# Attention scores of two units issued as one pair, and three waits elsewhere placed anew, in a one-core transformer kernel

## The chip, the cores and the metric

The kernel runs on one core of a Trainium2 chip. Its time is the device time of one launch in microseconds (us), from inputs in HBM to the output in HBM; smaller is better. Five engines work side by side, each on its own list of instructions: PE (TensorE, matrix products; PEld is its weight load), DVE (VectorE), ACT (ScalarE), POOL (GpSimd) and SP, which only issues DMAs. They wait for one another by semaphores.

## The reference, cut to what matters

Float32 throughout, 256 tokens of width 1024. Two layers, each a SwiGLU feed-forward, an attention block and a second SwiGLU; then a second block with a token mixer (mLSTM and gated linear attention) and a product-key expert layer.

```python
def hybrid_layer(x, ...):
    x = x + 0.5 * swiglu(rmsnorm(x, ffn1_norm), ffn1_w_gate, ffn1_w_up, ffn1_w_down)
    h = rmsnorm(x, mix_norm) @ w_in
    ...
    o_a = chunk_relpos_attention(a_q, a_k, a_v, a_rel_bias)      # 6 heads of 64
    o_b = dsa_attention(rope(b_q), rope(b_k), b_v, ...)          # 5 heads of 64, 64 keys selected a row
    o_c = mla_attention(c_q, c_kv, c_kr, ...)                    # 5 heads of 96
    x = x + concatenate([o_a, o_b, o_c]) @ w_out
    return x + 0.5 * swiglu(rmsnorm(x, ffn2_norm), ffn2_w_gate, ffn2_w_up, ffn2_w_down)

# each attention: s = q @ k.T * scale (+ bias or mask);  p = softmax(s);  o = p @ v
# token mixer, at its end: concatenate([sigmoid(ml_o) * head_rms(ml_h), silu(gla_r) * head_rms(gla_h)]) @ w_out
```

## The kernel before

**Matrix products.** To keep float32 accuracy each weight tile and each activation is split in a high and a low half: ACT writes the high half (`highs`, `high_part`, L272, L999), DVE the low half as the difference (`lows`, `low_part`, `low_half`, L284, L1008, L318), and PE makes three products (high by high, high by low, low by high; L326 to L328 and L1158 to L1160). Weights stream from HBM through five slots of `RAW` and two more places in `BIG`.

**The order of the work.** There is no scheduler. Each stage has one function for each engine, and their instructions stand as the code writes them. In the attention block all engines walk one list, `ORDER`, and each takes its own part of every entry.

**Attention.** The 16 heads are 16 units: 0 to 5 of kind A, 6 to 10 of kind C (98 rows deep), 11 to 15 of kind B (masked by a selection that DVE makes in eight rounds, L1214 to L1225). For a unit i the entries are:
- `score`: PE multiplies queries by keys into bank PB5 or PB4 (L1118, two products, 128 and 256 columns wide); DVE adds the bias and takes the maximum (L1294) or only takes it (L1292); ACT takes the exponential with its row sums (L1374);
- `norm`: DVE takes the reciprocal of the sums and scales the probabilities (L1303, L1307). For units 3 and 5 ACT does the scaling (L1371);
- `probs`: PE transposes the probabilities (L1132) and ACT copies them (L1382);
- `sum`, for every two units: PE multiplies by the values (L1143), ACT copies the high half (L1388), DVE takes the low half (L1312);
- `piece`: three products with the output weights (L1158 to L1160), up to three of them between two `probs`, to fill PE. `high` and `low` are halves of the output weights' tiles;
- `heads`: transposes of queries and keys by PE (L1102), copied out by ACT (L1363), 14 groups. For kinds A and B the queries of two heads lie in 128 rows. The copy is made twice, each time scaled by a column `HEAD_SCALE` that is 0.125 on 64 rows and 0 on the other 64, so that a product over 128 rows takes one head alone.

The `score` of unit i + 1 stands ahead of `norm` and `probs` of unit i. `HEADS_FOR` tells which groups a score waits for.

**First feed-forward.** For its first piece of 128 columns DVE scales the gate (L734), waits for ACT's SiLU (L818), multiplies (L738), splits (L742, L744), and PE starts the down product (L625). Between L734 and L738 DVE makes the low half of the first down tile, 2048 columns (`lows_upto(e, 3)`, L284).

**Token mixer, end.** `gla_vector` has, in this order, `update(4)`, the scaling of `OO` (L2369), `masked(1)` (L2341, for which PE's `own(1)`, L2269, waits), `update(5)`, `update(6)`, a half of the third output tile (`low_half(e, SECOND["out"][2], 1)`, L318) and `mix_turn_vector` (L2434). PE then multiplies by the output weights (`part`), the first time only when all four turned chunks are there.

Of the kernel before, what the change touches and what calls it, by code (L numbers as in the profile page):

```python
# [81 lines left out]
def build(nc, A, out):  # L82
    ctx = ExitStack()
    with ctx:
# [35 lines left out]
        HEAD_SCALE = COLS[:, 208:210]  # L120
# [252 lines left out]
        def setup_vector(e):  # L373
            e.memset(ONES[:, :], 1.0).then_inc(*ones_done.up())
            e.memset(NROW[:, :], NEG)
            e.memset(HEAD_SCALE, 0.0).then_inc(*v_step.up())
            e.wait_ge(*v_step.last())
            for x in range(2):
                e.memset(HEAD_SCALE[64 * x:64 * x + 64, x:x + 1], 0.125)
# [221 lines left out]

        def ffn_tensor(e, i):
# [12 lines left out]
            def down(f):  # L615
                w, c = FFN[i]["down"][f // 2], f % 3
                if f % 2 == 0:
                    tile_ready(e, w)
# [73 lines left out]
        def ffn_vector(e, i):  # L692
# [35 lines left out]
            for f in range(22):  # L728
# [6 lines left out]
                if i == 0 and f == 0:  # L735
                    lows_upto(e, 3)
# [9 lines left out]
                if i == 0 and f == 0:  # L746
                    condition_vector(e)
# [126 lines left out]
        AQ = Region(BIG, HN_AT, WB_AT)(6, 256)  # L874
        AQ_HALVES = AQ[:, 0:3, :], AQ[:, 3:6, :]
        BQ_HALVES = FREED[:, 0:3, :], FREED[:, 14:16, :]
# [26 lines left out]
        for dst, base, wide in ((AQ_HALVES, 0, True), (AK, 384, True), (CQ, 0, False), (CK, 0, False),  # L903
                                (BQ_HALVES, 1152, True), (BK, 1472, True)):
            if wide:
                for k0, k1 in ((0, 2), (2, 3)):
                    srcs = [H[:, b, base + k * 128:base + (k + 1) * 128] for k in range(k0, k1) for b in range(2)]
                    if dst is AK or dst is BK:
                        to = [(dst[:, k0:k1, :], 1.0)]
                    else:  # L910
                        to = [(half[:, k0:k1, :], HEAD_SCALE[:, x:x + 1]) for x, half in enumerate(dst)
                              if half.shape[1] >= k1]
                    HEADS.append((to, srcs))
# [10 lines left out]
        for h in range(6):  # L924
            PAIRS.append((AQ_HALVES[h % 2][:, h // 2, :], AK[:, h // 2, :],
# [4 lines left out]
        for h in (4, 0, 1, 2, 3):  # L930
            PAIRS.append((BQ_HALVES[h % 2][:, h // 2, :], BK[:, h // 2, :],
# [6 lines left out]
        HEADS_FOR = {6: 8, 7: 9, 9: 10}  # L938
# [6 lines left out]
        def turned_bank(i):  # L945
# [13 lines left out]
                4: [("heads", 6, 8), ("prod", 10, 1), ("heads", 8, 10)], 7: [("heads", 12, 14)]}  # L959
        NORMED_S = (3, 5)  # L960
# [3 lines left out]
        PIECES_AT = {5: 2, 6: 1, 7: 3, 8: 2, 9: 3, 10: 2, 11: 3, 12: 2, 13: 3, 14: 2, 15: 2}  # L964
# [4 lines left out]
        HIGH_AT = {7: (2, 0), 8: (2, 1), 10: (3, 0), 11: (3, 1), 12: (4, 0), 13: (4, 1), 14: (5, 0), 15: (5, 1)}  # L969
        LOW_AT = {5: (1, 0), 6: (1, 1), 10: (2, 0), 11: (2, 1), 12: (3, 0), 13: (3, 1), 14: (4, 0), 15: (4, 1)}  # L970
        pieces_ = []
        for i in range(NP):
            if i + 1 < NP:
                ORDER.append(("score", i + 1))
# [3 lines left out]
            if i > 0 and i % 2 == 0:  # L978
# [7 lines left out]
            ORDER.append(("probs", i))  # L986
            if i in HIGH_AT:
# [25 lines left out]
        def hybrid_tensor(e, l):  # L1013
# [3 lines left out]
            for what, *a in ORDER:  # L1017
# [86 lines left out]
                elif what == "score":  # L1104
                    i = a[0]
                    q, k, _, _, late = PAIRS[i]
                    if i == 0:
                        e.wait_ge(heads_read.sem, 14 * l + 4)
                    if i == 1:
                        e.wait_ge(scored.sem, 2 * l + 2)  # L1110
                        e.wait_ge(rest_in.sem, 32)
                    if i in HEADS_FOR:
                        e.wait_ge(heads_read.sem, 14 * l + HEADS_FOR[i])
                    if late:
                        e.wait_ge(heads_read.sem, 14 * l + 14)
# [57 lines left out]
        def hybrid_vector(e, l):  # L1173
# [55 lines left out]
            for what, *a in ORDER:  # L1229
# [48 lines left out]
                elif what == "score":  # L1278
# [6 lines left out]
                    if i - 1 in NORMED_S:  # L1285
                        e.wait_ge(att_exp.sem, base + i)
                        e.reciprocal(RECIP[:, (i - 1) % 2, :], EXPSUM[:, (i - 1) % 4, :])
# [12 lines left out]
                elif what == "norm" and a[0] not in NORMED_S:  # L1300
# [22 lines left out]
        def hybrid_scalar(e, l):  # L1323
# [6 lines left out]
            for what, *a in ORDER:  # L1330
# [34 lines left out]
                elif what == "score":  # L1365
                    i = a[0]
                    e.wait_ge(*att_shift.next())
                    if i - 1 in NORMED_S:
                        for b in range(2):
                            p = P_EXP[:, (i - 1) % 2, PART[b]]  # L1370
                            x = e.activation(p, p, ACT.Copy, scale=RECIP[:, (i - 1) % 2, b:b + 1])  # L1371
                        x.then_inc(*att_normed.up())
# [956 lines left out]
        def gla_vector(e):  # L2329
# [35 lines left out]
            update(4)  # L2365
            e.wait_ge(*rs_done.next())
# [91 lines left out]
        def mix_out_vector(e):  # L2458
# [29 lines left out]
            gate(0)  # L2488
            means(0)
# [4 lines left out]
            low_half(e, SECOND["out"][3], 1)  # L2494
            lower(0)
            scale(1)
            e.wait_ge(mixer_in.sem, 192)
# [32 lines left out]
        def mix_out_tensor(e):  # L2530
# [13 lines left out]
            for j in range(4):  # L2544
                if j < 3:
                    tile_ready(e, SECOND["out"][j])
                else:
                    e.wait_ge(first_low.sem, 5)
# [900 lines left out]
```

## Time and profile before

| what | value |
|---|---|
| median of 3 runs | 1921.29 us (1921.28 to 1921.61) |
| the profiled execution | 1921.31 us, of which the span from the first to the last instruction is 1919.5 us |
| mean granted TensorE clock | 0.994 |
| PE busy | 1781.0 us (93%) |
| DVE busy | 1385.5 us (72%) |
| ACT busy | 837.2 us (44%) |
| POOL busy | 303.1 us (16%) |
| chain that ended last | PE 66%, DMA 20%, DVE 9%, ACT 3% |
| the attention stages | about 275 to 342 us and 800 to 867 us |

Busy shares are means over stages with different limits: up to about 1262 us the kernel is held mostly by PE, behind it by the gathers of the expert layer. What a change is worth is read from the stage that it touches. A row of the timeline gives the start, the duration, and in brackets how long the engine had been idle and what ended that. The next instruction of an engine starts before the end that is recorded for the one before it, so what an instruction costs its queue is the step from its start to the next start.

### The profile page before, as it was taken

The numbers are of one execution on the slowest core, as the hardware profiler recorded it, in microseconds if no ns is written. First come the engines' busy times: TensorE is split into PE (matmuls) and PEld (weight loads), VectorE is DVE, ScalarE is ACT, GpSimd is POOL, SyncE is SP. The second block draws the span as 40 slices with busy tenths as digits, with TensorE's granted clock in tenths as the row PEclk, the third lists the DMA queues.
The fourth block names the chain that finished last, engine by engine and source line by source line (L and its number), as shares of the span: only waits on it lengthen the run. The fifth ranks groups of instructions, "written<-read, shape, count | busy, mean of one in ns | idle before, by whom it ended". The sixth has DMA issues, their size and how long they took to land.

```text
span 1919.5 us, 26939 instructions
## 1 busy us (share of the span) xinstructions
PE 1781.0 (93%) x10634; PEld 1408.4 (73%) x10634; DVE 1385.5 (72%) x2793; ACT 837.2 (44%) x1606; POOL 303.1 (16%) x341
## 2 busy tenths in 40 slices
PE   9999999999999999999999999989999877777776
PEld 8999997999999999969999899865555332222222
DVE  6787677779667876777787698877776577575745
ACT  6244456633353345575333654534533333333323
POOL 0000122000000002110000000033444333333330
PEclk9999999999999999999999999999999999999999
DMA  8666552567566755426775443399999999999997
GB/s 295 202 225 214 167 183 67 197 220 242 175 220 219 230 191 189 161 87 215 237 243 170 81 132 99 145 388 421 421 420 421 421 422 421 421 422 421 421 422 295
DMA packets 217654, 506.07 MB, mean 264 GB/s; under 512 B 10339, under 2 KB 167351, under 8 KB 183864
## 3 DMA queue, kind: packets, MB, share of 16 engines
q1 hardware_dynamic: 180376, 235.90, 37.4%
q0 software_dynamic: 37152, 268.45, 33.6%
q8 instruction: 84, 1.38, 0.3%
q14 instruction: 42, 0.34, 0.0%
HBM read 503.26 MB, written 1.06 MB: 263 GB/s over the span
## 4 chain that ended last, share of the span: by engine, by line
PE 66%; DMA 20%; DVE 9%; ACT 3%; issue 1%; another core or an unknown queue 0%; SPq 0%; DVEq 0%; ACTq 0%; POOLq 0%
PE PB L326 13%; PE PB L327 12%; PE PB L328 12%; DMA RAW<-in_c_experts,BIG 10%; PE PB L2793 6%; PE PB L625 4%; PE PB L627 4%; PE PB L626 4%; DMA HTF<-in_c_experts,BIG 4%; DMA BIG<-in_c_experts,BIG 3%; DMA HIF<-in_c_experts,BIG 2%; PE PB L2715 1%; DVE LOWS L284 1%; PE PB L1118 1%; DVE RAW L3057 1%
## 5 line engine op out<-in xcount | busy, mean ns | idle before, releaser
L284 DVE TENSOR_TENSOR LOWS<-RAW,HIGH 128x2048 fp32r<-128x2048 f32 (+2 forms) x131 | 301.0, 2306 | 32.1 <-ACT HIGH L272 31.5
L326 PE MATMUL PB<-HTR,HIGH 128*128 128x256 f32 (+1 forms) x1072 | 308.0, 287 | 0.4 <-DVE LOWS L304 0.4
L327 PE MATMUL PB<-HTR,HIGH 128*128 128x256 f32 (+1 forms) x1072 | 305.4, 285 | 0.0
L328 PE MATMUL PB<-HTR,LOWS 128*128 128x256 f32 (+1 forms) x1072 | 304.9, 284 | 0.0
L272 ACT ACTIVATE HIGH<-RAW 128x2048 fp32r<-128x2048 f32 (+3 forms) x138 | 263.8, 1920 | 51.0 <-DMA RAW<-in_ffn_w_up 23.6
L326 PEld LDWEIGHTS PB<-HTR,HIGH 128*128 128x128 f32 x1072 | 202.8, 189 | 4.5 <-DVE LOWS L304 0.6
L327 PEld LDWEIGHTS PB<-HTR,HIGH 128*128 128x128 f32 x1072 | 201.0, 188 | 3.6
L818 ACT ACTIVATE BIG<-BIG 128x256 f32<-128x256 f32 x88 | 36.7, 417 | 380.7 <-DVE BIG L734 380.7
L328 PEld LDWEIGHTS PB<-HTR,LOWS 128*128 128x128 f32 x1072 | 201.1, 188 | 2.1
L2793 PE MATMUL PB<-RAW,BIG 128*128 128x512 f32 x296 | 145.2, 621 | 47.9 <-ACT BIG L3163 47.9
L3152 ACT ACTIVATE BIG<-BIG 128x2 f32<-128x2 f32 (+1 forms) x132 | 26.8, 203 | 368.4 <-DVE BIG L3057 365.6
L2793 PE MATMUL PB<-HTF,BIG 128*128 128x512 f32 x304 | 142.7, 604 | 32.2 <-ACT BIG L3163 32.2
L326 PE MATMUL PB<-HIGH,HTR 128*128 128x280 f32 (+1 forms) x568 | 167.5, 295 | 1.7 <-DVE HTR L2483 0.8
L327 PE MATMUL PB<-LOWS,HTR 128*128 128x280 f32 (+1 forms) x568 | 164.0, 289 | 0.0
L328 PE MATMUL PB<-HIGH,HTR 128*128 128x280 f32 (+1 forms) x568 | 163.6, 288 | 0.0
L2793 PEld LDWEIGHTS PB<-RAW,BIG 128*128 128x128 f32 x296 | 54.4, 193 | 128.1 <-ACT BIG L3163 71.9
L2793 PE MATMUL PB<-HIF,BIG 128*128 128x512 f32 x292 | 138.1, 595 | 1.0 <-ACT BIG L3163 0.8
L3057 DVE CUSTOM_DVE_ANT_0 HIF<-HIF,PB 128x1024 f32<-128x1024 f32 x74 | 90.2, 1219 | 64.4 <-DMA HIF<-in_c_experts,BIG 64.3
L3057 DVE CUSTOM_DVE_ANT_0 RAW<-RAW,PB 128x1024 f32<-128x1024 f32 x75 | 91.5, 1220 | 62.2 <-DMA RAW<-in_c_experts,BIG 62.2
L2793 PEld LDWEIGHTS PB<-HTF,BIG 128*128 128x128 f32 x304 | 54.1, 190 | 107.2 <-ACT BIG L3163 57.3
L3057 DVE CUSTOM_DVE_ANT_0 HTF<-HTF,PB 128x1024 f32<-128x1024 f32 x76 | 92.1, 1219 | 53.7 <-DMA HTF<-in_c_experts,BIG 53.6
L326 PE MATMUL PB<-HTR,BIGR 128*128 128x256 f32 x384 | 110.1, 287 | 0.0
(488 smaller groups left out, 4042.9 us busy)
## 6 DMA issues: line engine op xcount, KB each, us to landing
RAW<-in_ffn_w_up SPq DMA_DIRECT2D x32, 1024.0 KB, 5.5
RAW<-in_ffn_w_down SPq DMA_DIRECT2D x32, 1024.0 KB, 5.1
RAW<-in_ffn_w_gate SPq DMA_DIRECT2D x31, 1024.0 KB, 5.4
RAW<-in_w_in SPq DMA_DIRECT2D x22, 1120.0 KB, 5.7
RAW<-in_w_mod SPq DMA_DIRECT2D x20, 1024.0 KB, 5.3
BIG<-in_ffn_w_gate SPq DMA_DIRECT2D x12, 1024.0 KB, 5.5
BIG<-in_ffn_w_up SPq DMA_DIRECT2D x12, 1024.0 KB, 8.4
BIG<-in_ffn_w_down SPq DMA_DIRECT2D x12, 1024.0 KB, 5.0
```

The costliest lines, as they stand in the source:

```text
L272: e.activation(u.h, u.raw, ACT.Copy).then_inc(*high_done.up())
L284: e.tensor_tensor(u.l, u.raw, u.h.bitcast(F32), ALU.subtract).then_inc(*low_done.up())
L326: e.matmul(o, lh, rh, start=k == 0, stop=False)
L327: e.matmul(o, lh, rl, start=False, stop=False)
L328: last = e.matmul(o, ll, rh, start=False, stop=k == len(ls) - 1)
L625: e.matmul(o, F_AH[:, c, s], w.h[:, f % 2, q], start=f == 0, stop=False)
L626: e.matmul(o, F_AH[:, c, s], w.l[:, f % 2, q], start=False, stop=False)
L627: last = e.matmul(o, F_AL[:, c, s], w.h[:, f % 2, q], start=False, stop=f == 21)
L818: e.activation(F_SG[:, c, :], F_SG[:, c, :], ACT.Silu).then_inc(*silu_done.up())
L2793: x = e.matmul(PB[4 * b + h][:, :], DIAG[:, g % 4, :], PLACES[PLACE_OF[g]][:, 1024 + h * 512:1536 + h * 512], start=g % 128 == 0, stop=g = ...
L3057: e.tensor_tensor_reduce(out=u, in0=u, in1=H2[b], scale=1.0, scalar=0.0, op0=ALU.mult, op1=ALU.add, accum_out=AV[:, b, c:c + 1]).then_inc( ...
L3152: e.activation(AV[:, b, c:c + n], AV[:, b, c:c + n], ACT.Gelu).then_inc(*s_step.up())
```

## The change

In the attention blocks:
- the entry `score` of unit i + 1 no longer stands ahead of `norm` of unit i. From unit 2 on, the scores of units i + 1 and i + 2 (i odd) stand together behind `probs` of unit i: PE issues both units' 128-column products and then both units' 256-column products, and DVE and ACT take the two units one after the other;
- queries of kinds A and B are copied once, with the factor 0.125, and each unit multiplies on its own 64 rows (`PAIRS`, the slice `r`): rows 0 to 63 for the even head, 64 to 127 for the odd. `HEAD_SCALE` goes;
- DVE normalizes units 3 and 5 too (`NORMED_S` goes);
- `heads` 12 and 13 move from unit 7 to unit 6, one `sum` into the filling of unit 4, and pieces, `high` and `low` are dealt out anew.

In the first feed-forward the low half of the first down tile is made in two parts, one ahead of the wait for the factors, one behind the first split. In the mixer `masked(1)` stands ahead of the wait for `rs_done`, the half of the third output tile comes later, in `mix_out_vector`, the second half of the fourth as well, and PE's first `part` waits for one turned chunk at a time.

```diff
+        def first_down(e, x):
+            t = FFN[0]["down"][0]
+            ...
+            e.wait_ge(high_done.sem, t.splits)
+            e.tensor_tensor(t.l[:, x, :], t.raw[:, x, :], t.h[:, x, :].bitcast(F32),
+                            ALU.subtract).then_inc(*(low_done if x else first_low).up())
...
+            else:
+                first_down(e, 0)
             e.wait_ge(*rstd_full.next())
...
-                if i == 0 and f == 0:
-                    lows_upto(e, 3)
                 e.wait_ge(*silu_done.next())
...
                 if i == 0 and f == 0:
+                    first_down(e, 1)
                     condition_vector(e)
...
+            r = slice(64 * (h % 2), 64 * (h % 2) + 64)
+            PAIRS.append((AQ[r, h // 2, :], AK[r, h // 2, :],
...
-        HEADS_FOR = {6: 8, 7: 9, 9: 10}
+        HEADS_FOR = {6: 9, 8: 10, 10: 14}
...
-        NORMED_S = (3, 5)
...
-        PIECES_AT = {5: 2, 6: 1, 7: 3, 8: 2, 9: 3, 10: 2, 11: 3, 12: 2, 13: 3, 14: 2, 15: 2}
+        PIECES_AT = {5: 2, 6: 1, 7: 3, 8: 3, 9: 2, 10: 3, 11: 2, 12: 3, 13: 2, 14: 3, 15: 1}
...
-            if i + 1 < NP:
-                ORDER.append(("score", i + 1))
+            if i == 0:
+                ORDER.append(("score", 1))
...
             ORDER.append(("probs", i))
+            if i == 6:
+                ORDER.append(("heads", 12, 14))
+            if i % 2 and i + 1 < NP:
+                ORDER += [("scores", i + 1), ("score", i + 1), ("score", i + 2)]
...
                     for b in range(2):
-                        o = score_bank(i)[:, PART[b]]
-                        last = e.matmul(o, q[:, b * 128:(b + 1) * 128], k[:, 0:128 * (b + 1)], start=True, stop=True)
-                    last.then_inc(*att_scored.up())
+                        for i in units:
+                            q, k = PAIRS[i][0:2]
+                            last = e.matmul(score_bank(i)[:, PART[b]], q[:, b * 128:(b + 1) * 128], k[:, 0:128 * (b + 1)],
+                                            start=True, stop=True)
+                            if b:
+                                last.then_inc(*att_scored.up())
...
             update(4)
+            masked(1)
             e.wait_ge(*rs_done.next())
...
-            masked(1)
             update(5)
             update(6)
-            low_half(e, SECOND["out"][2], 1)
             mix_turn_vector(e)
...
             gate(0)
+            low_half(e, SECOND["out"][2], 1)
             means(0)
...
                 if j == 0:
-                    e.wait_ge(ht_low.sem, 8 * turn_count["p"] + 4)
-                part(0, j, 0, 4)
+                    for k in range(4):
+                        e.wait_ge(ht_low.sem, 8 * turn_count["p"] + k + 1)
+                        part(0, j, k, k + 1)
+                else:
+                    part(0, j, 0, 4)
```

DVE in the first feed-forward, from the copy of the factors on, before (the 2048-wide row is the low half of the first down tile):

```order
L715 COPY BIG<-PB3 128x256
L734 TENSOR_TENSOR BIG<-PB2,BIG 128x256
L284 TENSOR_TENSOR LOWS<-RAW,HIGH 128x2048
L738 TENSOR_TENSOR BIG<-PB3,BIG 128x256
L742 CAST BIGR<-BIG 128x256
L744 TENSOR_TENSOR BIGR<-BIG,BIGR 128x256
L386 COPY CT<-COLS 128x16
```

and now:

```order
L603 TENSOR_TENSOR LOWS<-RAW,HIGH 128x1024
L723 COPY BIG<-PB3 128x256
L742 TENSOR_TENSOR BIG<-PB2,BIG 128x256
L744 TENSOR_TENSOR BIG<-PB3,BIG 128x256
L748 CAST BIGR<-BIG 128x256
L750 TENSOR_TENSOR BIGR<-BIG,BIGR 128x256
L603 TENSOR_TENSOR LOWS<-RAW,HIGH 128x1024
L381 COPY CT<-COLS 128x16
```

One row of 2048 columns between the two products with PB2 and PB3 became two rows of 1024, ahead of the copy and behind the split.

ACT in the attention block, from the exponential of unit 13 (before) and of unit 12 (now) to the copy of unit 13's transposed probabilities. `BIG,SM` rows are exponentials, `HIGH` a half of an output tile, `HTR<-PB3` the high half of the sum of units 10 and 11, `BIG<-PB3` a copy of transposed probabilities. Before:

```order
L1374 ACTIVATE BIG,SM<-PB2,SM 128x128
L1374 ACTIVATE BIG,SM<-PB2,SM 128x256
L1388 ACTIVATE HTR<-PB3 128x256
L1382 ACTIVATE BIG<-PB3 128x384
L999 ACTIVATE HIGH<-RAW 128x1024
L1374 ACTIVATE BIG,SM<-PB2,SM 128x128
L1374 ACTIVATE BIG,SM<-PB2,SM 128x256
L1382 ACTIVATE BIG<-PB3 128x384
```

and now:

```order
L1371 ACTIVATE BIG,SM<-PB2,SM 128x128
L1371 ACTIVATE BIG,SM<-PB2,SM 128x256
L1371 ACTIVATE BIG,SM<-PB2,SM 128x128
L1371 ACTIVATE BIG,SM<-PB2,SM 128x256
L1004 ACTIVATE HIGH<-RAW 128x1024
L1385 ACTIVATE HTR<-PB3 128x256
L1379 ACTIVATE BIG<-PB3 128x384
L1004 ACTIVATE HIGH<-RAW 128x1024
L1379 ACTIVATE BIG<-PB3 128x384
```

Now two exponentials and a half of an output tile stand ahead of the copy of the sum, where one exponential stood.

DVE at the same place, from the normalization of unit 12 on (reciprocal and two scalings; `ISA` rows are the bias and maximum of a score, `HTR<-PB3` the low half of the sum). Before:

```order
L1303 RECIPROCAL SM<-SM 128x2
L1307 TENSOR_SCALAR BIG<-BIG,SM 128x128
L1307 TENSOR_SCALAR BIG<-BIG,SM 128x256
L1312 TENSOR_TENSOR HTR<-PB3,HTR 128x256
L1008 TENSOR_TENSOR LOWS<-RAW,HIGH 128x1024
L1294 ISA PB2,SM<-PB2,BIG 128x128
L1294 ISA SM 128x1
L1294 ISA PB2,SM<-PB2,BIG 128x256
L1294 ISA SM 128x1
L1303 RECIPROCAL SM<-SM 128x2
L1307 TENSOR_SCALAR BIG<-BIG,SM 128x128
L1307 TENSOR_SCALAR BIG<-BIG,SM 128x256
```

and now:

```order
L1305 RECIPROCAL SM<-SM 128x2
L1309 TENSOR_SCALAR BIG<-BIG,SM 128x128
L1309 TENSOR_SCALAR BIG<-BIG,SM 128x256
L1314 TENSOR_TENSOR HTR<-PB3,HTR 128x256
L1013 TENSOR_TENSOR LOWS<-RAW,HIGH 128x1024
L1305 RECIPROCAL SM<-SM 128x2
L1309 TENSOR_SCALAR BIG<-BIG,SM 128x128
L1309 TENSOR_SCALAR BIG<-BIG,SM 128x256
L1013 TENSOR_TENSOR LOWS<-RAW,HIGH 128x1024
```

The score of unit 14 no longer stands between the low half of the sum and the normalization of unit 13; the low half of an output tile still does.

## Rows read from the trace of the kernel before

**Rows 1.** Busy time by stage, the first hybrid attention (columns as the first line has them).
```profile
core 0: us, PE busy (x) PEld busy (x) DVE busy (x) ACT busy (x) POOL busy (x), PEclk, DMA share, GB/s
...
275.00:342.00 67.00, 63.09 (x398) 50.42 (x398) 51.95 (x173) 47.89 (x121) 10.49 (x8) 1.00 0.29 95
```

**Rows 2.** Chain that ended last, first feed-forward (start us, us, what).
```profile
21.15 2.20 DVE LOWS L284
...
24.62 0.47 PE PB L625
...
27.63 0.12 PE PB L326
```

**Rows 3.** Timeline, ACT then DVE, first feed-forward (start us, us, what, [idle before]).
```profile
17.54 1.90 ACT L272 ACTIVATE HIGH<-RAW 128x2048 fp32r<-128x2048 f32 x1
...
24.47 4.49 DVE L284 TENSOR_TENSOR LOWS<-RAW,HIGH 128x2048 fp32r<-128x2048 f32 x2
...
29.77 0.43 DVE L738 TENSOR_TENSOR BIG<-PB,BIG 128x256 f32<-128x256 f32 x1 [0.48 <-ACT BIG L818]
```

**Rows 4.** Timeline of PE in the first hybrid attention.
```profile
294.02 0.87 PE L1143 MATMUL PB<-BIG 128*64 128x256 f32 x8 [0.92 <-ACT BIG L1382]
...
309.03 0.47 PE L1158 MATMUL PB<-HIGH,BIGR 128*128 128x512 f32 x1 [1.74 <-ACT HTF L1363]
...
323.74 0.82 PE L1118 MATMUL PB<-HTF 128*128 128x128 f32 x4
...
324.49 0.87 PE L1143 MATMUL PB<-BIG 128*64 128x256 f32 x8
...
326.79 0.49 PE L1132 MATMUL PB<-CST,BIG 128*128 128x128 f32 x3
...
327.11 0.82 PE L1118 MATMUL PB<-HTF 128*128 128x128 f32 x4
...
330.95 0.87 PE L1143 MATMUL PB<-BIG 128*64 128x256 f32 x8
```

**Rows 5.** Timeline of DVE there, around unit 13 (325.30 and 325.50 normalize unit 12).
```profile
324.70 0.30 DVE L1294 CUSTOM_DVE_ANT_0 PB<-PB,BIG 128x128 f32<-128x128 f32 x1 [0.50 <-PE PB L1118]
...
325.30 0.16 DVE L1303 RECIPROCAL SM<-SM 128x2 f32<-128x2 f32 x1
...
325.50 0.55 DVE L1307 TENSOR_SCALAR BIG<-BIG,SM 128x128 f32<-128x128 f32 x2
...
326.70 0.42 DVE L1312 TENSOR_TENSOR HTR<-PB,HTR 128x256 fp32r<-128x256 f32 x1 [0.65 <-ACT HTR L1388]
...
327.04 1.22 DVE L1008 TENSOR_TENSOR LOWS<-RAW,HIGH 128x1024 fp32r<-128x1024 f32 x1
...
328.17 0.29 DVE L1294 CUSTOM_DVE_ANT_0 PB<-PB,BIG 128x128 f32<-128x128 f32 x1
```

**Rows 6.** Timeline of ACT there: two pieces of it.
```profile
311.41 1.05 ACT L999 ACTIVATE HIGH<-RAW 128x1024 fp32r<-128x1024 f32 x1
...
312.36 0.36 ACT L1374 ACTIVATE BIG<-PB,SM 128x128 f32<-128x128 f32 x1
...
325.48 0.37 ACT L1374 ACTIVATE BIG<-PB,SM 128x128 f32<-128x128 f32 x1
...
326.29 0.38 ACT L1388 ACTIVATE HTR<-PB 128x256 fp32r<-128x256 f32 x1
```

**Rows 7.** Timeline of PE: the index scores on 32 rows, and what follows.
```profile
261.67 1.15 PE L1084 MATMUL PB<-BIG 32*128 32x256 f32 x16
...
262.74 0.40 PE L326 MATMUL PB<-HIGH,HTR 128*128 128x280 f32 x1
```

**Rows 8.** Timeline, PE then DVE, end of the token mixer.
```profile
1227.03 2.05 PE L2269 MATMUL PB<-BIG 128*128 128x128 f32 x16 [0.79 <-DVE BIG L2341]
...
1237.66 0.60 PE L2540 MATMUL PB<-CST,BIG 128*128 128x128 f32 x4
...
1228.93 1.23 DVE L318 TENSOR_TENSOR LOWS<-RAW,HIGH 128x1024 fp32r<-128x1024 f32 x1
```

More of the change, by code:

```diff
@@ L375, in setup_vector @@
             e.memset(NROW[:, :], NEG)
[L376 to L379, printed above, removed]
             e.memset(HALF[:, :], 0.0).then_inc(*v_step.up())
@@ L600, in mods_at @@
             return MODS[i][j - 3], f % 2
+        def first_down(e, x):
+            t = FFN[0]["down"][0]
+            assert made["low"] == t.n
+            if x:
+                made["low"] += 1
+            e.wait_ge(high_done.sem, t.splits)
+            e.tensor_tensor(t.l[:, x, :], t.raw[:, x, :], t.h[:, x, :].bitcast(F32),
+                            ALU.subtract).then_inc(*(low_done if x else first_low).up())
         def ffn_tensor(e, i):
@@ L902, in build @@
         HEADS = []
-        for dst, base, wide in ((AQ_HALVES, 0, True), (AK, 384, True), (CQ, 0, False), (CK, 0, False),
-                                (BQ_HALVES, 1152, True), (BK, 1472, True)):
+        for dst, base, wide in ((AQ, 0, True), (AK, 384, True), (CQ, 0, False), (CK, 0, False),
+                                (BQ, 1152, True), (BK, 1472, True)):
             if wide:
@@ L907, in build @@
                     srcs = [H[:, b, base + k * 128:base + (k + 1) * 128] for k in range(k0, k1) for b in range(2)]
[L908 to L913, printed above, removed]
+                    HEADS.append(([(dst[:, k0:k1, :], 0.125 if dst is AQ or dst is BQ else 1.0)], srcs))
             else:
@@ L958, in build @@
         FILL = {0: [("prod", 9, 0)], 1: [("prod", 9, 1)], 2: [("prod", 10, 0)], 3: [("begin", 10, 1), ("heads", 4, 6)],
[L959 to L960 removed]
+                4: [("heads", 6, 8), ("sum", 1), ("prod", 10, 1), ("heads", 8, 10)]}
         BEGUN = [tuple(a) for f in FILL.values() for what, *a in f if what == "begin"]
         SELECT_AT = {0: (0,), 1: (1,), 2: (2,), 3: (3,), 4: (4,), 6: (5,), 7: (6,), 8: (7,)}
[L964 removed]
+        PIECES_AT = {5: 2, 6: 1, 7: 3, 8: 3, 9: 2, 10: 3, 11: 2, 12: 3, 13: 2, 14: 3, 15: 1}
         PIECE_ORDER = {0: [], 1: [("piece", m, 1, h) for m in range(2) for h in range(2)] +
@@ L977, in build @@
                 pieces_ += PIECE_ORDER[(i - 3) // 2]
-            if i > 0 and i % 2 == 0:
+            if i > 0 and i % 2 == 0 and i != 4:
                 ORDER.append(("sum", i // 2 - 1))
@@ L1103, in hybrid_tensor @@
                         last.then_inc(*heads_turned.up())
[L1104 to L1107, printed above, removed]
+                elif what == "scores" or (what == "score" and a[0] < 2):
+                    units = (a[0], a[0] + 1) if what == "scores" else (a[0],)
+                    if a[0] == 0:
                         e.wait_ge(heads_read.sem, 14 * l + 4)
-                    if i == 1:
+                    if a[0] == 1:
                         e.wait_ge(scored.sem, 2 * l + 2)
                         e.wait_ge(rest_in.sem, 32)
[L1112 to L1115, printed above, removed]
+                    if a[0] in HEADS_FOR:
+                        e.wait_ge(heads_read.sem, 14 * l + HEADS_FOR[a[0]])
                     for b in range(2):
-                        o = score_bank(i)[:, PART[b]]
-                        last = e.matmul(o, q[:, b * 128:(b + 1) * 128], k[:, 0:128 * (b + 1)], start=True, stop=True)
-                    last.then_inc(*att_scored.up())
+                        for i in units:
[4 more added lines that the diff above has]
+                                last.then_inc(*att_scored.up())
                 elif what == "probs":
@@ L1299, in hybrid_vector @@
                         selection(r_)
-                elif what == "norm" and a[0] not in NORMED_S:
+                elif what == "norm":
                     i = a[0]
@@ L1367, in hybrid_scalar @@
                     e.wait_ge(*att_shift.next())
[L1368 to L1372, printed above, removed]
                     for b in range(2):
@@ L2493, in mix_out_vector @@
             means(1)
-            low_half(e, SECOND["out"][3], 1)
             lower(0)
             scale(1)
+            low_half(e, SECOND["out"][3], 1)
             e.wait_ge(mixer_in.sem, 192)
```

22 lines of the change are left out of this document (9 added, 13 removed).

## Prediction

> **What bounds the kernel now.** I read the stage table first, since the busy shares are means. In the first attention stage PE is busy 63.09 of 67.00 us [rows 1]: it holds the stage, and all its waits together are 3.9 us. The page has PE on 66% of the chain that ended last, and it stays the bound up to the gathers behind 1262 us. So what the change brings or costs is PE's idle time, plus any change in PE's own steps. Then I read the chain and the timelines at the three places of the change. In the first feed-forward the chain leaves PE: a DVE row of 2.20 us stands in it, and PE's down product starts at 24.62 [rows 2]. In the attention PE has two large waits, 0.92 at 294.02 and 1.74 at 309.03, and from unit 8 on hardly any [rows 4]. At the end of the mixer PE waits 0.79 for a DVE mask [rows 8].
>
> The sum is made against the profiled execution, 1921.31 us, which is the median (1921.29) to 0.02. From no change a measurement of this kernel tells about 0.2%, so faster means below 1917.4 and slower above 1925.1.
>
> **First feed-forward.** The row of 2.20 goes from between DVE's two products [rows 2]. Its first half, 1.13 by the step of a row of that size (327.04 to 328.17, [rows 5]), can start when ACT's high half ends, 17.54 + 1.90 = 19.44 [rows 3], and ends at 20.6. DVE was idle there, but the copy of the factors comes some 0.4 later for it. What is late next is the SiLU, which the row of 2.20 had covered: where nothing covers it, DVE waits 0.48 for it behind a product of about 0.42, so 0.9 (the row at 29.77, [rows 3]). At L738 the sum is 23.35 (the end of 21.15 + 2.20) - 2.20 + 0.4 + 0.5, where 0.5 is the part of the 0.9 that isn't the product itself: 22.05. PE starts the down product 1.3 earlier, at 23.3. It doesn't keep all of it. The down product ends 3.0 later (27.63 - 24.62, [rows 2]), at 26.3, and the gate tile behind it needs its low half, which on DVE now stands behind the second half. Before, that low half was made from 24.47, 2.2 long (4.49 for two, [rows 3]), to 26.7, hidden. Now it starts at 24.47 - 1.3 + 1.13 = 24.3 and ends at 26.5, so PE goes on at 26.6 where it was at 27.63. Gain 1.0. The bounds are 0.3 (if all of the 1.13 is paid again) and 1.3. PE is the bound from here on, so it is carried through.
>
> **Attention, what goes.** Numbers are of the first layer; the second has the same list.
> - The wait of 1.74 [rows 4] is a piece of unit 7 that came right behind heads 12 and 13, whose copies ACT had to finish. They move one unit ahead. -1.7.
> - The wait of 0.92 at the first sum [rows 4], with ACT's copy at its end. The sum moves into the filling of a later unit, behind pieces. -1.1 with the smaller wait behind it (from both sides: 0.5 and 1.3).
> - Scores on 64 rows. A score now is four products, 128 and 256 columns twice, on 128 rows, and costs 0.75 (323.74 to 324.49, [rows 4]). A pair of them costs 1.5. No row shows 64 rows. The nearest are the index scores on 32: 16 products of 256 columns in 1.07 (261.67 to 262.74, [rows 7]), where 0.75 for 768 columns makes 4.0 for those 4096. That is 3.7 times as fast with four row groups, so they run side by side. For two groups I take that a pair costs 0.9 and saves 0.6; the bounds are 0 (nothing side by side) and 0.75 (a full half). Only pairs of kinds A and B have both groups, 2/3, 4/5, 12/13 and 14/15: the pairs with unit 6 to 10 save nothing, 10/11 with them. -1.2 ahead of unit 8, -1.2 behind.
> - One copy for a group of queries instead of two, and no memsets for `HEAD_SCALE`: nothing, ACT is busy 47.89 of 67.00 [rows 1] and PE doesn't wait there, once the 1.74 is gone. If that cover is gone too, it is a gain.
>
> What comes new ahead of unit 8: unit 3 is normalized on DVE behind a selection round and not on ACT, and the first piece waits for heads 9. I estimate 0.8 for each, about the size of the wait of 0.92 that an ACT copy left, between 0 and 1.6. With -0.3 for the smaller waits around unit 5 the part up to unit 7 makes -1.7 - 1.1 - 1.2 - 0.3 + 1.6 = -2.7. The score of unit 8 stands no longer in this part but in the next (-0.7 here): -3.4.
>
> **Attention, what comes: a loop through three engines.** Before, the score of unit i + 1 stood a whole unit ahead of the transposes that need it. Now both scores of a pair are issued behind unit i's transposes, and those of unit i + 2 must be through DVE and ACT one unit of PE's later. The order shows what stands between: on ACT two exponentials and a half tile ahead of the copy of the sum, and on DVE the low half of the sum and a half tile ahead of the second normalization. One turn, from the start of a pair's scores to the start of the next pair's:
> - score start to DVE's end, 323.74 to the next row on DVE at 324.70, 0.96 (up to the start of the maximum), and from there to the exponential 0.78 (to 325.48) [rows 4 to 6];
> - the exponentials, a step of 0.81 each (325.48 to 326.29, [rows 6]), 1.62; the half tile, 0.95 (311.41 to 312.36, [rows 6]);
> - the copy of the sum until DVE takes it, 0.41 (326.29 to 326.70), the low half 0.34 (to 327.04), the half tile 1.13 (to 328.17) [rows 5, 6];
> - the normalization 0.75 (325.30 to 325.50, and 0.55, [rows 5]), about 0.1 for PE to take it up, the transposes 0.32 (326.79 to 327.11, [rows 4]).
>
> Together 7.4. Before, two units took 6.46 from score to score (324.49 to 330.95 by the sums behind them, [rows 4]), held by PE; with side-by-side scores PE's own work would be 5.9. So the loop is longer than the work and PE waits 1.5 a turn, mostly at the transposes of units 9, 11 and 13. Pair 8/9 has no overlap and a selection round on DVE in place of the half tile; I take 8.2. Loss: 8.2 + 7.4 + 7.4 - 3 x 6.46 = 3.6 to the scores of 14/15, and 0.3 behind them, 3.9.
>
> Net for a layer: -3.4 + 3.9 = +0.5, for both +1.0. From both sides: if half of the new waits don't come, -2.9 a layer; if the row groups don't overlap, +2.4 a layer more (four pairs, 0.6 each), less where the loop hides it.
>
> A rule of the Trainium skill speaks against the scores on 64 rows. TensorEngine Tiling (Array Packing), section Key Properties, says that a change of the tiling mode, not of the tile alone, drains TensorE. The trace shows a switch out of 32 rows at 262.74, where the product behind took 0.40 as recorded, and the 16 products took 1.07 with the switch in them [rows 7]; that leaves no room for a drain of more than some 0.1. By the rule each of the seven pairs and the first scores would pay at entry and exit, 16 a layer and 3.2 us in all at 0.1; the forecast would be 1923.4, still within 0.2%.
>
> **Mixer, end.** With `masked(1)` ahead of the scaling, PE's `own(1)` doesn't wait 0.79 [rows 8]. DVE's half tile at 1228.93, 1.23 long [rows 8], goes from ahead of the turned chunks' input; PE's transposes at 1237.66 [rows 8] come up to 1.3 earlier. Then the half tiles stand ahead of the output's updates and I give back 0.2. Gain 1.1, bounds 0.3 (only part of it reaches the chain) and 1.4 (nothing given back); the gathers behind start earlier by as much.
>
> **Sum.** 1921.31 - 1.0 + 1.0 - 1.1 = 1920.2.
>
> **Rivals.**
> - A, the forecast: large waits in front go, a loop behind takes their place, 1920.2. Chance 0.6. For it: the lengths of the loop are all rows. Against: it is a chain of means, and a step of 0.3 in it counts six times.
> - B, the loop doesn't hold PE: PE's pieces between two `probs` cover it, and the new waits of 3.9 are half or less, -2.9 a layer on top. 1921.31 - 1.0 - 1.1 + 2 x (-2.9 + 0.5) = 1914.4; with no new waits at all, 2 x -3.4 in place of +1.0, 1912.4. Chance 0.25. For it: ACT and DVE have 19 and 15 us without work in the stage [rows 1]. Against: work is missing there, order isn't.
> - C, slower: the two groups of 64 rows don't run side by side. Then PE's own work stays 6.46 a turn, less of it waits, and four pairs a layer give back 0.6: 1920.2 + 4.8 = 1925.0, and above 1925.1 where a drain or one more late copy of 0.1 comes to it; it decides from a pair's cost of 1.5 on. Chance 0.12. Against: 32 rows overlap [rows 7].
> - D, the edits elsewhere bring nothing, since later waits take them up: 1921.31 + 1.0 = 1922.3. Chance 0.03.
>
> **Numbers.** A lies within 0.2% but for a tenth. B is faster nearly always. C is half slower. Faster 0.28, the same 0.63, slower 0.09. The range reaches to B with halved waits and to C: 1914.4 to 1925.0; A's own is 1917.0 to 1923.5.
>
> **What would show it.** In the trace of the changed kernel: the down product of the first feed-forward at 23.3, and the gate tile behind it at 26.6 after a short wait for DVE. No wait over 0.5 at the first sum and behind heads 12 and 13. A pair of scores of kind A or B in 0.9 from start to next start; 1.5 makes it C. Waits of 1 to 2 us for DVE's normalization at the transposes of units 9, 11 and 13, idle time of the stage about 8 us instead of 3.9; 5 or less makes it B. `own(1)` without a wait, and the mixer's transposes some 1.2 nearer to it. The prediction is wrong if the stage's length changes by more than 2.5 us, or if the two stages differ by more than 1.

## The result, and the profile after

The changed kernel took 1926.79 us (median of 7 runs, 1925.29 to 1929.25), before 1921.31 in the same session; ratio 1.0028, 95% interval 1.0018 to 1.0037. It is slower by 5.5 us, against a forecast of 1920.2, 1.1 faster. The profiled execution (1926.79 us, span 1925.0) is the median. Beside the loss the spread is wide: 4.0 from lowest to highest, where the 7 executions of before have 0.6 (18 to 27 of them in later sessions 1.4 to 2.9, without one execution of 4529 us, which no ratio counts).

The two small edits did what was forecast. PE in the first feed-forward (start us, us, engine, line, what, [idle before <- what ended it]):

```profile
23.11 0.47 PE L631 MATMUL PB<-HIGH,BIGR 128*128 128x512 f32 x1 [0.25 <-DVE BIGR L750]
26.43 0.39 PE L325 MATMUL PB<-HTR,HIGH 128*128 128x256 f32 x1 [0.30 <-DVE LOWS L283]
```

The down product starts at 23.11 where it started at 24.62 [rows 2], and the gate tile behind it waits 0.30 for DVE's low half: on the timeline of before that tile started at 27.47, so the gain is 1.04. Some of it is lost again further on: the last index scores of the first layer start 0.95 earlier than before. At the mixer's end:

```profile
1232.65 2.05 PE L2266 MATMUL PB<-BIG 128*128 128x128 f32 x16
```

`own(1)` has no wait (0.79 in [rows 8]). PE's last transposes of the mixer's output stand 5.08 later than in [rows 8] (1242.74 against 1237.66), while PE had come into the mixer 6.48 later (1214.92 to 1221.40, both on PE's timelines). The gain there is about 1.1 by the landmark behind it (1254.23 to 1259.63, 5.40 later).

So all the loss is in the two attention stages. From the last index scores of a layer to the first transposes behind its pieces, before took 80.3 in both. The change took 82.8 in the first and 85.1 in the second. The first stage, PE, by its waits and the scores:

```profile
291.19 0.55 PE L1137 MATMUL PB<-CST,BIG 128*128 128x128 f32 x3 [1.11 <-DVE BIG L1309]
...
297.41 0.47 PE L1163 MATMUL PB<-HIGH,BIGR 128*128 128x512 f32 x1 [0.51 <-ACT HTF L1365]
...
307.35 1.48 PE L1121 MATMUL PB<-HTF 98*128 98x128 f32 x8
308.75 0.87 PE L1148 MATMUL PB<-BIG 128*64 128x256 f32 x8
...
315.33 0.55 PE L1137 MATMUL PB<-CST,BIG 128*128 128x128 f32 x3 [1.70 <-DVE BIG L1309]
315.72 2.06 PE L1121 MATMUL PB<-HTF 98*128 98x128 f32 x8
317.70 0.87 PE L1148 MATMUL PB<-BIG 128*64 128x256 f32 x8
...
323.13 0.55 PE L1137 MATMUL PB<-CST,BIG 128*128 128x128 f32 x3 [0.55 <-DVE BIG L1309]
323.61 0.93 PE L1121 MATMUL PB<-HTF 64*128 64x128 f32 x8
324.46 0.87 PE L1148 MATMUL PB<-BIG 128*64 128x256 f32 x8
...
330.70 0.55 PE L1137 MATMUL PB<-CST,BIG 128*128 128x128 f32 x3 [0.84 <-DVE BIG L1309]
331.18 0.93 PE L1121 MATMUL PB<-HTF 64*128 64x128 f32 x8
...
336.47 0.50 PE L1163 MATMUL PB<-HIGH,BIGR 128*128 128x512 f32 x1 [0.94 <-DVE BIGR L1314]
```

The whole first layer, before and then with the change (columns: stretch and length, busy time of PE, PEld, DVE, ACT and POOL, granted clock, DMA share, GB/s):

```profile
261.67:341.99 80.32, 76.41 (x518) 62.79 (x517) 64.33 (x206) 54.55 (x132) 10.49 (x8) 1.00 0.34 115
260.72:343.50 82.78, 76.40 (x518) 60.59 (x517) 66.21 (x210) 50.34 (x125) 9.90 (x8) 1.00 0.32 111
```

PE's busy time is the same, 76.41 and 76.40. The scores on 64 rows made PE's work no shorter, and the whole 2.46 is more idle time, 6.38 where it was 3.91. (The ends of PE's rows are modelled, and the first two scores, from 273.41 on, are one row of 1.91, so a short gap can be hidden in it.)

The large waits of [rows 4] are gone. In their place PE waits for DVE at the transposes of units 3, 9, 11 and 13, and at a piece behind unit 14. A pair of scores on 64 rows takes 0.85 (323.61 to 324.46), the pair 8/9 on 98 rows 1.40, and the mixed pair 10/11 takes 1.98 (315.72 to 317.70).

The second stage has the same waits, but for the one at unit 11, and something more. Stretches of 4 us (columns as above), and PE's timeline there:

```profile
840.00:844.00 4.00, 2.30 (x13) 1.54 (x12) 3.78 (x13) 1.78 (x3) 0.00 (x0) 1.00 0.81 259
844.00:848.00 4.00, 4.00 (x13) 1.99 (x14) 1.93 (x9) 1.89 (x9) 0.00 (x0) 0.51 0.00 2
848.00:852.00 4.00, 4.00 (x14) 3.15 (x14) 2.18 (x5) 1.39 (x3) 0.00 (x0) 0.64 0.00 0
```

```profile
842.77 0.55 PE L1137 MATMUL PB<-CST,BIG 128*128 128x128 f32 x3 [1.70 <-DVE BIG L1309]
843.15 2.95 PE L1121 MATMUL PB<-HTF 98*128 98x128 f32 x8
846.04 1.55 PE L1148 MATMUL PB<-BIG 128*64 128x256 f32 x8
```

Behind the wait of 1.70 the granted clock goes to 0.51, which is the lower of TensorE's two levels (1.2 GHz): the same pair takes 2.89 and not 1.98, the sum behind it 1.47 and not 0.80. The layer is 2.33 longer for it, net of the wait at unit 11 that it hides. Before has a wait of 1.74 in the first stage [rows 4] and of 1.73 in the second, and no such stretch in either. Behind about 1280 us, where the kernel is held by the gathers, every profiled execution has such stretches, before's too (a granted clock of 0.50 from 1612 to 1616, for instance); the counts below are for the attention stages only.

### The profile page after: what moved, and what is told of

Same layout as the page of the kernel before. It is cut to its first block, busy times and chain, and to the rows that moved or that the text cites. A ratio compares the mean times of both kernels' runs of the same rounds, so it can differ in the third digit from the quotient of the medians.

```text
span 1925.0 us, 26932 instructions
## 1 busy us (share of the span) xinstructions
PE 1789.2 (93%) x10634; PEld 1409.0 (73%) x10634; DVE 1388.9 (72%) x2799; ACT 829.5 (43%) x1592; POOL 303.3 (16%) x341
## 4 chain that ended last, share of the span: by engine, by line
PE 64%; DMA 20%; DVE 10%; ACT 5%; issue 1%; another core or an unknown queue 0%; SPq 0%; DVEq 0%; ACTq 0%
PE PB L325 12%; PE PB L326 12%; PE PB L327 12%; DMA RAW<-in_c_experts,BIG 10%; PE PB L2793 6%; PE PB L631 4%; PE PB L633 4%; PE PB L632 4%; DMA HTF<-in_c_experts,BIG 4%; DMA BIG<-in_c_experts,BIG 3%; DMA HIF<-in_c_experts,BIG 2%; PE PB L2715 1%; ACT BIG L1371 1%; DVE LOWS L283 1%; DVE RAW L3057 1%
```

## Experiments

Times are medians, with the ratio to the kernel before and its interval. "Layer" is the length measured as above, first and second, in the profiled execution. Which side of the change costs was asked first: each part alone.

**The two small edits alone.** The attention hunks of the diff are taken back.

> The kernel before with only the two small edits of the change: the first feed-forward and the end of the mixer. The attention stays as it was. The trace of the change shows PE 1.04 ahead behind the first feed-forward (27.47 to 26.43) and 1.08 gained in the mixer. If these two are worth what they show and the attention is all that was lost: 1921.3 - 2.1 = 1919.2, with a spread as small as that of before (0.6 from lowest to highest). Rival: the gains in front are taken up by later waits or the clock falls for another reason than the attention: 1921 or more.

1919.56 (1919.2 to 1920.05), ratio 0.9992 (0.9983 to 1.0001), layers 80.3 and 80.3. At the landmark behind the mixer PE is 1.90 earlier than before (1252.33 for 1254.23), and 1.6 arrives at the end, against 2.1 forecast. The gain is not clear of noise by itself, but the spread is small and the loss is not here.

**The attention part alone.** The hunks of the feed-forward and of the mixer are taken back.

> The kernel before with the attention part of the change alone. The two other edits alone gained 1.6. If the parts add up: 1926.8 + 1.6 = 1928.4, with the spread of 3 to 4 of the changed kernel, each attention stage 2.4 longer than before and one or both longer still by a slow stretch of TensorE's clock. If the slow clock came from where the edits moved the stages in time: a small spread and 1926.1 (1921.3 + 2 x 2.4).

1929.03 (1927.80 to 1931.01), ratio 1.0041 (1.0027 to 1.0055). The parts add up to about 0.4: 7.4 for this part and -1.6 for the other make 5.8, and the change measured 5.5. Here the slow stretch stood in the first stage (layer 83.6, granted clock 0.87 and 0.70 at 316 to 324) and none in the second (82.8): it belongs to neither layer. It cost only 0.76, where the one in the change's second stage cost 2.33.

**The change once more**, unedited.

> The changed kernel once more, unedited, for the spread of its times beside the run with two filler products (1924.2 to 1926.3 in 11 runs). If idle time in the loop lets the clock fall in most executions, but not in all: a median of 1926.8 again, single times down to 1924.4 (no slow stretch in the attention) and up to 1929. If the first runs only met a bad moment: a median near 1924.5.

1926.60 (1924.90 to 1930.02), ratio 1.0028. Its profiled execution, of 1928.67 us, had a slow stretch in both stages, each behind the wait at unit 9, and layers of 85.1 and 85.1:

```profile
312.00:316.00 4.00, 2.30 (x13) 1.58 (x12) 3.59 (x13) 1.93 (x5) 0.00 (x0) 1.00 0.81 262
316.00:320.00 4.00, 4.00 (x15) 2.16 (x15) 2.12 (x10) 2.11 (x10) 0.00 (x0) 0.61 0.02 4
320.00:324.00 4.00, 4.00 (x13) 3.05 (x12) 2.18 (x5) 1.12 (x2) 0.00 (x0) 0.54 0.00 0
```

**Work in the wait.** Theory: the clock falls for the idle time. Rival: it falls for something else. Products of a constant by a constant, which nothing uses, fill PE's wait at unit 9:

```diff
                 elif what == "probs":
                     i = a[0]
+                    if i == 9:
+                        e.wait_ge(ot_low.sem, 8 * l + i // 2)
+                        for x in range(6):
+                            e.matmul(PB[7][:, 0:384], IDENT, CST[:, 0:384], start=True, stop=True)
                     e.wait_ge(*att_normed.next())
```

> The changed kernel with six products of 128x384 (an identity with constants, into the bank that the transposes then overwrite) ahead of PE's wait for unit 9's probabilities, in both attention layers. In the changed kernel PE is idle 1.70 there, and in the second layer the granted clock is 0.51 to 0.64 for some 8 us right behind it. The products fill about 1.5 of the 1.7 and shorten nothing else. If the idle time brings the clock down: no clock under 1.0 in the stage, the second layer as long as the first, time 1926.8 - 2.4 = 1924.4. If the clock falls for another reason (the power drawn before, the state of the chip): it falls here too, 1926.8.

1928.05 (1927.63 to 1929.83), ratio 1.0039 (1.0025 to 1.0053). I had mis-sized the work: six products lasted 3.87, not 1.5, and each layer took 84.7. But no stretch of either stage had a clock under 1.00 in the profiled execution. With `range(2)`:

> As the filler before, with two products of 128x384 and not six: in that run each took 0.64, so that six lasted 3.87 and lengthened each layer. Two last 1.3 of the 1.7 that PE waits there and shorten nothing. If the idle time in front of unit 9's transposes is what brings the clock down in some executions: no granted clock under 1.0 in either stage, both layers of one length, and the time is the changed kernel's 1926.8 less the 2.4 of its slow stretch, 1924.4, with a small spread. If the fall is independent of it: 1926 to 1927 with a spread of 3 or so as in the changed kernel.

1924.92 (1924.17 to 1926.32), ratio 1.0016 (1.0007 to 1.0026), layers 82.8 and 82.8. The wait is 0.41 and the clock stays:

```profile
313.92 1.45 PE L1130 MATMUL PB<-CST 128*128 128x384 f32 x4
315.77 0.55 PE L1141 MATMUL PB<-CST,BIG 128*128 128x128 f32 x3 [0.41 <-DVE BIG L1313]
```

Work that computes nothing and shortens nothing took 1.7 to 1.9 off the median and half of the spread: of the 15 executions of the change 13 took longer than the longest with two filler products (1926.32). The loss of order, without the clock, is 2.5 a layer.

**Which part of the loop.** Theory: PE waits at units 9, 11 and 13 since the chain through ACT and DVE is longer than PE's work; the half tiles in it are what can go. Rival: DVE's load holds it. Both half tiles moved:

```diff
-        HIGH_AT = {7: (2, 0), 8: (2, 1), 9: (3, 0), 10: (3, 1), 11: (4, 0), 12: (4, 1), 13: (5, 0), 14: (5, 1)}
-        LOW_AT = {6: (1, 0), 7: (1, 1), 9: (2, 0), 10: (2, 1), 11: (3, 0), 12: (3, 1), 13: (4, 0), 15: (4, 1)}
+        HIGH_AT = {8: (2, 1), 10: (3, 1), 12: (4, 1), 14: (5, 1)}
+        HIGH_BEHIND_SUM = {8: (2, 0), 10: (3, 0), 12: (4, 0), 14: (5, 0)}
+        LOW_AT = {6: (1, 0), 7: (1, 1), 9: (2, 0), 11: (3, 0), 13: (4, 0), 15: (4, 1)}
+        LOW_BEHIND_SCORES = {9: (2, 1), 11: (3, 1)}
```

> The changed kernel with the half tiles of the output weights taken out of the loop through ACT and DVE: on ACT the high half stands behind the copy of the sum and not ahead of it, on DVE one of two low halves stands behind the maxima of a pair and not between the sum and the second normalization. The loop gets 0.95 and 1.13 shorter, 7.4 to 5.3 by the rows, PE's own work being 5.9. If the loop holds PE: the waits at units 9, 11 and 13 (1.70, 0.55, 0.84) go nearly all, the clock doesn't fall, 1926.8 - 2.4 - 2 x 3.0 = 1918.4. Rival: it is DVE's load (5.7 of work a turn) and not the order that holds it, so that half of the waits stay: 1921.4 or more.

1917.51 (1917.05 to 1919.16), ratio 0.9982 (0.9973 to 0.9991), layers 79.3 and 79.3: 3.5 less each, and no slow stretch. PE waits 0.75 at unit 9 and 0.22 at 13. The rival, with 1921.4 or more, falls. Then each engine's part alone.

> The changed kernel with only ACT's part of the shorter loop: the high half of a tile stands behind the copy of the sum and not ahead of it. Both parts together took each attention layer from 82.8 (no slow stretch) to 79.3. If the loop is one chain through both engines, 0.95 goes from each of three turns (the wait at unit 9 from 1.70 to about 0.75, the others, 0.55 and 0.84, nearly away), and the piece at unit 15 waits less: a layer of 80.3 and, since the slow stretch followed the long wait, none or few of them: 1917.5 + 2 x 1.0 = 1919.5. If DVE's low half alone held it: no gain but the spread, 1925 to 1926.

1917.85 (1917.39 to 1918.84), ratio 0.9981 (0.9972 to 0.9990), layers 79.4 and 79.4. ACT's part alone gives nearly all. Why can be read in the changed kernel's own rows, ACT and then DVE, between unit 12's exponential and unit 13's normalization:

```profile
326.26 0.37 ACT L1371 ACTIVATE BIG<-PB,SM 128x128 f32<-128x128 f32 x1
...
327.05 1.07 ACT L1004 ACTIVATE HIGH<-RAW 128x1024 fp32r<-128x1024 f32 x1
328.00 0.40 ACT L1385 ACTIVATE HTR<-PB 128x256 fp32r<-128x256 f32 x1
```

```profile
326.60 0.55 DVE L1309 TENSOR_SCALAR BIG<-BIG,SM 128x128 f32<-128x128 f32 x2
328.43 0.42 DVE L1314 TENSOR_TENSOR HTR<-PB,HTR 128x256 fp32r<-128x256 f32 x1 [1.28 <-ACT HTR L1385]
328.77 1.22 DVE L1013 TENSOR_TENSOR LOWS<-RAW,HIGH 128x1024 fp32r<-128x1024 f32 x1
329.90 0.16 DVE L1305 RECIPROCAL SM<-SM 128x2 f32<-128x2 f32 x1
330.10 0.55 DVE L1309 TENSOR_SCALAR BIG<-BIG,SM 128x128 f32<-128x128 f32 x2
```

DVE is idle for 1.28 until ACT's copy of the sum comes, which stands behind a high half of 0.95; behind it are the low half of the sum, a low half tile and only then the reciprocal and scaling of unit 13, whose transposes PE waits for. With the high half behind the copy:

```profile
314.24 0.55 PE L1140 MATMUL PB<-CST,BIG 128*128 128x128 f32 x3 [0.75 <-DVE BIG L1312]
...
327.90 0.55 PE L1140 MATMUL PB<-CST,BIG 128*128 128x128 f32 x3 [0.41 <-DVE BIG L1312]
...
334.91 0.87 PE L1151 MATMUL PB<-BIG 128*64 128x256 f32 x8 [0.21 <-ACT BIG L1382]
```

The wait at unit 9 went from 1.70 to 0.75, by the length of the half tile; the one at 13 went from 0.84 to 0.41, and the one at 11 and the one at the piece (0.94) are gone.

> The changed kernel with only DVE's part of the shorter loop: one of two low halves stands behind the maxima of a pair and not between the sum and the second normalization. The pair 8/9's turn has a selection round there and not this half, so that the wait of 1.70 at unit 9 stays (and with it slow stretches in some executions), and only the waits at 11 and 13 (0.55, 0.84) go: a layer of 81.4, time 1926.8 - 2 x 1.4 = 1924.0, with a wide spread. If ACT's half alone held the loop: 1926.8.

1925.09 (1920.25 to 1926.77), ratio 1.0013 (1.0004 to 1.0022), layers 81.0 and 80.9 in a profiled execution of 1920.87. The wait at unit 9 stays:

```profile
315.44 0.55 PE L1140 MATMUL PB<-CST,BIG 128*128 128x128 f32 x3 [1.72 <-DVE BIG L1312]
```

The eleven times fall into two heaps, five of 1920.25 to 1922.74 and six of 1925.09 to 1926.77. The mean granted clock of the whole execution is 0.991 to 0.995 in the lower heap and 0.988 to 0.990 in the upper, so slow stretches are the likely difference. It isn't shown where they stood, since only an execution of the lower heap was profiled. Moving DVE's half shortens the loop by 1.8 a layer, but it doesn't take the long wait away, and so the median shows little of it.

**Scores on 64 rows.** The mixed pair, unit after unit, not in turns:

```diff
-                    for b in range(2):
-                        for i in units:
+                    apart = a[0] == 10
+                    for x, y in [(i, b) for i in units for b in range(2)] if apart else [(i, b) for b in range(2) for i in units]:
+                        for i, b in ((x, y),):
```

> The changed kernel, where the products of units 10 (98 rows) and 11 (64 rows) are issued one unit after the other, and not in turns. In the changed kernel this pair takes 1.98 from its start to the next start, the pair 8/9 (both 98 rows) 1.40, the pairs on 64 rows 0.85. If each change between 98 and 64 rows costs PE about 0.2, with three fewer... two of three changes gone the pair takes 1.2 to 1.5 and each layer gains 0.4 to 0.6: 1925.8. If the pair takes long for another reason (a wait for a bank or for heads): still 1.98, 1926.8.

1925.24 (1923.49 to 1926.55), ratio 1.0020 (1.0011 to 1.0029), layers 82.3 and 82.4. The pair takes 1.61 (315.56 to 317.17 below), 0.37 less than in turns, for two of three changes between 98 and 64 rows: about 0.18 a change. The layers are 0.4 shorter.

```profile
315.56 1.67 PE L1122 MATMUL PB<-HTF 98*128 98x128 f32 x8
317.17 0.87 PE L1149 MATMUL PB<-BIG 128*64 128x256 f32 x8
```

All pairs unit after unit (the same edit with no condition):

> The changed kernel, where the products of the two units of every pair are issued one unit after the other: the slices of 64 rows stay, but neighbouring products use the same rows except at one place of the pair. If row groups run side by side only when they alternate: a pair of kind A or B takes 1.3 to 1.5 instead of 0.85; the pair 10/11 1.6 as with that pair alone apart. The first unit's maximum can start earlier, which the loop through ACT and DVE likes: between 1925.2 (the run with 10/11 alone apart) - 1 and + 2. If the slices of 64 rows are fast by themselves, the pairs stay at 0.85.

1924.01 (1923.10 to 1925.66), ratio 1.0012 (1.0003 to 1.0022), layers 82.2 and 82.9 (one slow stretch in the second, which cost 0.74). The second forecast came: a pair on 64 rows still takes 0.86.

```profile
330.50 0.93 PE L1121 MATMUL PB<-HTF 64*128 64x128 f32 x8
331.36 0.87 PE L1148 MATMUL PB<-BIG 128*64 128x256 f32 x8
```

That could mean that 64 rows are cheap by themselves. The next run says no: the order of before, the two small edits, and only the slices of 64 rows.

```diff
-            PAIRS.append((BQ_HALVES[h % 2][:, h // 2, :], BK[:, h // 2, :],
+            r = slice(64 * (h % 2), 64 * (h % 2) + 64)
+            PAIRS.append((BQ[r, h // 2, :], BK[r, h // 2, :],
```

> The kernel before with the two small edits and, of the attention part, only the slices of 64 rows (queries of kinds A and B copied once, each unit multiplied on its own half); the order of all entries is that of before, with no pairs. In the runs so far a pair on 64 rows took 0.85 whether its products alternated between the halves or not, against 1.5 for two units on 128 rows. If a score on 64 rows is cheaper by itself, each of the 11 units of kinds A and B takes about 0.43 instead of 0.75, the attention stages get up to 3.5 shorter each where PE holds them, at least the four to six units behind unit 10 count: 1919.6 - 2 x (1.5 to 3.5) = 1912.6 to 1916.6. If the gain needs two halves issued next to each other: scores stay at 0.7 or more and the time at 1919.6 or, with single switches between 64 and 128 rows, above.

1925.70 (1923.85 to 1928.51), ratio 1.0024 (1.0015 to 1.0033), layers 82.5 and 82.5, 2.15 more each than with the small edits alone. That is the second forecast (no gain without two halves, and a cost where the row size switches), with a cost that it had left open; PE's busy time in the first layer is 79.03, against 76.44 with the small edits alone. One unit on 64 rows, and then the same score on 128 rows in the kernel before:

```profile
327.82 0.92 PE L1120 MATMUL PB<-HTF 64*128 64x128 f32 x4
328.67 0.50 PE L1160 MATMUL PB<-HIGH,HTR 128*128 128x512 f32 x1
```

```profile
327.11 0.82 PE L1118 MATMUL PB<-HTF 128*128 128x128 f32 x4
327.58 0.58 PE L1158 MATMUL PB<-HIGH,HTR 128*128 128x512 f32 x1
```

It takes 0.85, as long as a pair does. On 128 rows the same score let the next product start after 0.47. So the second unit of a pair on the other half adds no time, even when the two are issued one after the other, and one unit alone is dearer than on 128 rows: by 0.2 ahead of a `sum` (0.85 for 0.75, and 0.42 for 0.33 from the transposes to the score), by 0.4 ahead of a piece. By the Trainium skill (TensorEngine Tiling (Array Packing), Key Properties) a change of tiling mode drains TensorE. These runs agree that a change costs time, about 0.18 us by the mixed pair.

**The best of it.** The shorter loop with the mixed pair apart.

> The kernel with the shorter loop, and units 10 and 11 issued one after the other. Alone the shorter loop gave 1917.5 and the other edit took 0.37 off the pair's step (1.98 to 1.61) in each layer. If PE holds the stage in the shorter loop, both add up: 1917.5 - 0.8 = 1916.7. If the loop still holds it at unit 9 to 11 (PE waited 0.75 there): 1917.5.

1916.76 (1916.28 to 1917.85), ratio 0.9975 (0.9965 to 0.9984), layers 78.9 and 78.9. The savings add, and the version beats both kernels: 4.8 under before, 10.0 under the change (that one measured in another session).

## Why the prediction was wrong

- *First feed-forward, gain 1.0; mixer, gain 1.1*: right, 1.04 and 1.08, by the mechanisms given (SiLU uncovered, the low half behind). Rival D falls, though of the first gain 0.2 is lost again before the mixer, and of the 2.1 together 1.6 arrived at the end.
- *What goes in front of unit 8, -3.4*: right in the waits and wrong in the work. From the last index scores to the score that starts the turns (before unit 9's, at 310.82, with the change the pair 8/9, at 307.35) the layer is 2.5 shorter, 46.63 for 49.15. PE's idle time there fell by 1.48, as forecast (-1.5), with new waits of 1.11 and 0.51 where I took 0.8 and 0.8. Its busy time fell by 1.04 and not by 1.9 (1.2 for two pairs on 64 rows, 0.7 for unit 8's score, which now stands behind this point).
- *The loop's turns, 8.2, 7.4 and 7.4*: 8.37, 7.89 and 7.57 (307.35, 315.72, 323.61, 331.18), where before took 19.37 for three (310.82 to 330.19). The chain was right and its links are those forecast. The excess is 0.8, and 0.5 of it is the turn of the mixed pair: I had that pair at the cost of two scores of before, and it took 1.98.
- *Behind the scores of 14/15, 0.3*: 0.5, 12.32 for 11.80 (331.18 to 343.50, 330.19 to 341.99). I hadn't seen the wait of 0.94 at the piece, where before waits 0.30 near the end: its low half waits for the same late copy of the sum.
- *The scores on 64 rows*: the failed step in PE's work. The sum had -1.2 for them in front of unit 8, and PE's own work at 5.9 for 6.46 a turn behind it; the layer's busy time went from 76.41 to 76.40. A pair costs 0.85, as forecast (0.9), but two scores of before cost 0.75 and 0.58, not 1.5: the 0.75 was read where a `sum` follows, and ahead of a piece the next product starts after 0.47 and is itself late by 0.1. Coming to a pair from the transposes costs 0.1 more than before (0.42 for 0.33), so that a pair saves about 0.4 and not 0.6. That would make 1.6 a layer. The mixed pair gives back 0.65 of it, and the first two scores, issued singly on 64 rows, up to 0.5 (1.84 from 273.41 to 275.25; before 1.65 from 274.27 to 275.92 with a wait of 0.27 in it); the pairs on 98 rows (1.40) save nothing, and where the last 0.5 goes I haven't traced. This is where the rule of the Trainium skill that I weighed was right and my reading of [rows 7] too low for these products: I left "no room for a drain of more than some 0.1", and by the mixed pair a change costs near 0.18, paid three times in it.
- *The clock*: the other failed step, since it had no term. I read the granted clock of the stage as given (1.00 in [rows 1]) and asked of each new wait only how long PE stands. The slow stretch of the profiled execution, which is the median, cost 2.33.

Together: 1920.2, and 2 x (0.9 + 0.8 + 0.2) for the order and the scores, and 2.3 for the clock, 1926.3; of the 0.5 that is left, 0.2 is what the first feed-forward's gain lost on its way, and 0.3 I can't place. Of the rivals none came. B fell, since the loop does hold PE; C fell, since two halves do overlap. The idle time of the layer was 6.4, between the "about 8" of the forecast and the 5 of B, so the forecast of 0.5 a layer had too much idle time in it and too little work.

Of the cause it is shown that the loss is in the attention, that ACT's half tile ahead of the copy of the sum makes the waits (1.70 to 0.75 when moved), and that neither filler nor shorter loop has a slow stretch where it was profiled. Open is what else the clock asks. In 12 stages with a wait of 1.5 to 1.7 at unit 9, profiled in this study, 5 had a slow stretch behind it; three of them cost 2.3 and two 0.75. In 10 with 0.8 or less there or with work in it, none had; in the 6 stages in the order of before, with a wait of 1.7 to 2.1 in another place, also none, though the wide spread of the run with half rows makes it likely that other executions of it had some. And with two filler products times still spread over 2.1.

## What to carry to other kernels

When two steps are merged so that a producer is issued later, write down the whole chain through the other engines from issue to use, and take out of it what only fills (here a half tile of 0.95 ahead of a copy that two engines wait for): it was worth 9 us of 1927, the slow stretches included. Price a product by what follows and precedes it, since the same score cost 0.75 in one place and 0.58 in another, and check a forecast saving against the engine's busy time over the whole stage. And a wait on PE can cost more than its length: look at the granted clock behind it, and at the spread of the runs, which shows it before a profile does.

## What the runs showed of the hardware

- Products on rows 0 to 63 and on 64 to 127 overlap on PE whether they alternate or not: 0.85 and 0.86 for the scores of a pair, 0.85 for one unit alone.
- A change between products on 128 or 98 rows and on 64 rows costs PE about 0.18 us (1.98 for the mixed pair with three changes, 1.61 with one); a single score on 64 rows is 0.2 to 0.4 dearer than one on 128.
- TensorE's granted clock fell to the lower level behind waits of 1.5 to 1.7 us in 5 of 12 stages, and not in a fixed layer. A fall made the stage 2.3 us longer three times and 0.75 twice.
